# Second attention: the scores of two heads issued together on the two halves of TensorE's rows

## The chip, the cores and the metric

The kernel runs on one NeuronCore of a Trainium2 chip. The time is the device time of one execution in microseconds (us), the median of three runs. Everything is float32 at the inputs and outputs.

## The reference

Two transformer blocks in a row on 256 tokens of width 1024. The first has a short convolution, a feed-forward layer, a latent attention (MLA) and another feed-forward layer. The second, whose mixer is touched here, projects the tokens to a gated linear attention (GLA) and to a grouped-query attention (GQA), and goes on with a mixture of 64 experts. Cut to the part that matters:

```python
ATT_HEADS, ATT_KV_HEADS, ATT_HEAD_DIM = 8, 2, 64     # heads 0..3 share key head 0, heads 4..7 key head 1

def gqa_group(q, k, v, q_gain, k_gain, out_gain):
    qh = rms_norm_2(heads(q), q_gain); kh = rms_norm_2(heads(k), k_gain); vh = heads(v)
    qh = apply_axial_rope(qh, cos, sin) * (dh ** -0.5); kh = apply_axial_rope(kh, cos, sin)
    s = einsum('bkgqd,bksd->bkgqs', qb, kh)           # per head: 256 x 256 scores, no mask
    p = softmax(s, axis=-1)
    o = einsum('bkgqs,bksd->bkgqd', p, vh)
    return rms_norm_2(o.reshape(B, T, 512), out_gain)

h = h + concat(gla_group(...), gqa_group(...)) @ w_out
h = h + hier_moe(rms_norm_2(h, norm2_gain), ...)      # 64 experts, 3 matrices of 2 MB each
return rms_norm_2(h, final_gain)
```

## The kernel before, in words

Each engine has one instruction queue, written out by hand, and runs it in order. Engines meet only at semaphores. TensorE is PE, VectorE DVE, ScalarE ACT, GpSimd POOL; all large loads are issued by SyncE (SP), in a fixed order too.

The queries of the second attention lie transposed in SBUF: 128 partitions by four blocks of 256 tokens. Block `c` holds head `c` in partitions 0 to 63 and head `c + 4` in partitions 64 to 127. The keys lie in `KT` the same way, key head 0 in the lower half of the partitions and key head 1 in the upper. `slot(hd)` gives block and half of a head. A "head" below is the loop's number t or v; it runs from 0 to 7.

For each head the work is a chain over three engines:

1. `scores(t)` (PE, L1673): two matmuls, 64 rows deep, 256 columns wide, into PSUM bank `t % 2`. So two heads' scores can exist at once.
2. the maxima (DVE, L1828 and L1829), a reduction over both token tiles and a scaling; they signal `amax`.
3. the exponentials (ACT, L1768), one for each token tile with the row sums beside; they signal `aexps`, which also frees the bank.
4. `turned` (PE, L1682): four transposes of the probabilities into bank 2, and their copy to SBUF (ACT, L1780), which signals `apt_read`.
5. `weighted` (PE, L1691): four matmuls with the values into bank 3. After four heads DVE divides by the sums (L1806, L1808) and signals `oa`; the fifth head's `weighted` waits for that.

In PE's loop (`gqa_pe`) iteration t waits for `aexps` of t, then issues `scores(t + 1)`, `turned(t - 1)` and `weighted(t - 2)`.

The GLA's work is written in between these steps, on all engines. On PE: `gla_kv_pe` (L1394) in iteration 2, which waits for a copy on ACT (L1785); `gla_own_pe` (L1403), which waits for DVE's states (L1635, L1639), and `gla_past_pe` (L1418) in iteration 3; `gla_out_pe` (L1426), which waits for DVE's gated output, in iteration 6. On ACT, iteration 4 has the exponentials of head 4, then the copy of what `gla_past_pe` left (L1774, "past_read"), then the copy of head 3's probabilities, then eight squares (L1790), which wait for DVE's sum (L1650, "osum"). On DVE, iteration 4 has the maximum of head 4, then the low part of an output weight (`pair_lo(0)`, L268), then that sum (L1650), which waits for "past_read". DVE's iteration 6 has the maximum of head 6, then the GLA means (L1815), the gated output (L1821), and the division for the first four heads.

From iteration 7 on PE also computes the output projection (`part_out`, L317 to L319), which needs the GLA's operand from DVE and ACT (L564, L556). Its completed parts free the weight slots.

SP issues the experts' weights (2 MB each, `moe_sp`, L2179) in the order of slots 0, 3, 7, 2, 1, 4, 5, 8, 6, 9, each after a wait for the slot's last reader: slot 2 waits for "osum", slot 1 for the first output-projection part (`used` of `part_out(0, 0, 1)`), slot 4 for the last transposes of `turned_on`. After these the queue refills a slot whenever PE has read it.

Of the kernel before, what the change touches and what calls it, by code (L numbers as in the profile page):

```python
# [16 lines left out]
ALU = mybir.AluOpType  # L17
# [3 lines left out]
P = 128  # L21
T = 256
# [15 lines left out]
AH, AKV, AD = 8, 2, 64  # L38
# [81 lines left out]
def program(nc, a, consts_d, out):  # L120
    sems, chained = {}, {}

    def s(name):
        name = chained.get(name, name)
        if name not in sems:
            sems[name] = nc.alloc_semaphore(name)
        return sems[name]
# [38 lines left out]
    def sb(name, shape, dt=F32):  # L166
        return nc.alloc_sbuf_tensor(name, shape, dt)
# [39 lines left out]
    work = sb("work", [P, WORK])  # L207
    h = sb("h", [P, TT, D])
    small = sb("small", [P, 248])
# [24 lines left out]
    def wk(at, n):  # L234
        assert at + n <= WORK
        return work[:, at:at + n]

    def bank(b, n=512, at=0):
        return ps[:, b, at:at + n]
# [185 lines left out]
    def dve_step(dve, ins):  # L425
        steps["dve"] += 1
        ins.then_inc(s("dve_steps"), 1)
        dve.wait_ge(s("dve_steps"), steps["dve"])
# [858 lines left out]
    GQ, GK, GV, SG, ZT, QK, AV = 2048, 2560, 3072, 4096, 5120, 5632, 6912  # L1287
# [368 lines left out]
    QT, KT, PB2, PT2, OA, ON = 0, ZT, 1024, 2048, 3072, 0  # L1656

    def xw(at, n):

        return x_slots[:, at:at + n]  # L1660

    def slot(hd):

        return hd % 4, hd // 4

    P_BANK, O_BANK, OG_BANK, ON_BANK = 2, 3, 4, 0

    def gqa_pe(pe):
        def scores(t):
            c, par = slot(t)  # L1670
            rows = slice(64 * par, 64 * par + 64)
            for tt in range(TT):
                last = pe.matmul(bank(t % 2, T, T * tt), xw(QT, 1024)[rows, T * c + P * tt:T * c + P * tt + P],  # L1673
                                 work[rows, KT:KT + T], start=True, stop=True, skip_group_check=True)
            last.then_inc(s("ascores"), 1)

        def turned(v):
            if v:
                pe.wait_ge(s("apt_read"), v)
            for kk in range(TT):  # L1680
                for tt in range(TT):
                    last = pe.transpose(bank(P_BANK, P, T * kk + P * tt), xw(PB2 + 512 * (v % 2) + T * tt + P * kk, P), ident)  # L1682
            last.then_inc(s("aprobs_T"), 1)

        def weighted(v):
            pe.wait_ge(s("apt_read"), v + 1)
            if v == 4:
                pe.wait_ge(s("oa"), 1)
            for tt in range(TT):
                for kk in range(TT):  # L1690
                    last = pe.matmul(bank(O_BANK, AD, T * tt + AD * (v % 4)), xw(PT2 + 512 * (v % 2) + T * kk + P * tt, P),  # L1691
                                     wk(AV + P * kk + AD * (v // 4), AD), start=kk == 0, stop=kk == 1, skip_group_check=True)
            last.then_inc(s("aatt"), 1)

        def w_out(q):
            by_token(pe, U_WOUT + q, ACC, oT, [2 * q, 2 * q + 1], 2, D, 512, q == 0, q == 3,
                     between=first_rows(pe, "mix", "n2") if q == 3 else None).then_inc(s("used"), 1)

        def part_out(q, tt, part):
            unit_ready(pe, U_WOUT + q)  # L1700
            hi, lo = weights(U_WOUT + q, 2, D)
            cs = slice(512 * part, 512 * part + 512)
            for i, ch in enumerate((2 * q, 2 * q + 1)):
                last = passes(pe, ACC[tt][part], oT[0][:, ch, tt * P:(tt + 1) * P], oT[1][:, ch, tt * P:(tt + 1) * P],
                              hi[:, i, cs], lo[:, i, cs], q == i == 0, False)
            return last

        def turned_on():
            pe.wait_ge(s("on"), 1)
            for c in range(4):  # L1710
                for tt in range(TT):
                    last = pe.transpose(bank(ON_BANK + c // 2, P, (c % 2) * T + P * tt), xw(ON + 512 * tt + P * c, P), ident)
                if c % 2:
                    last.then_inc(s("on_T"), 1)

        pe.wait_ge(s("akt"), 1)
        scores(0)
        scores(1)
        gla_scores_pe(pe)
        gla_keys_pe(pe)  # L1720
        keep_busy(pe, 2, P_BANK)
        for t in range(1, AH + 1):
            pe.wait_ge(s("aexps"), t)
            if t + 1 < AH:
                scores(t + 1)
            if t == 2:
                gla_kv_pe(pe)
            turned(t - 1)
            if t == 6:
                gla_out_pe(pe)  # L1730
            if t >= 2:
                weighted(t - 2)
            if t == 3:
                gla_own_pe(pe)
                gla_past_pe(pe)
            if t == 7:
                pe.wait_ge(*mark("og_lo", 1))
                pe.wait_ge(*mark("past_read", 1))
                part_out(0, 1, 0)
        part_out(0, 1, 1)  # L1740
        weighted(AH - 1)
        pe.wait_ge(*mark("og_lo", 2))
        part_out(0, 0, 0)
        part_out(0, 0, 1).then_inc(s("used"), 1)
        part_out(1, 1, 0)
        part_out(1, 1, 1)
        turned_on()
        part_out(1, 0, 0)
        part_out(1, 0, 1).then_inc(s("used"), 1)
        pe.wait_ge(*mark("mo_lo", 2))  # L1750
        w_out(2)
        w_out(3)
# [47 lines left out]
    def gqa_dve(dve):  # L1800
        def weighted(half):

            dve.wait_ge(s("aatt"), 4 * half + 4)
            sums = small[:, 128 + 16 * half:144 + 16 * half].rearrange("p (h c) -> p h c", c=4)[:, :, 2:4]
            inv = small[:, 112 + 8 * half:120 + 8 * half].rearrange("p (h c) -> p h c", c=2)
            dve_step(dve, dve.reciprocal(inv, sums))  # L1806
            for tt in range(TT):
                last = dve.tensor_tensor(xw(OA + 512 * tt + 256 * half, 256).rearrange("p (h c) -> p h c", c=AD),  # L1808
                                         bank(O_BANK, T, T * tt).rearrange("p (h c) -> p h c", c=AD),
                                         inv[:, :, tt:tt + 1].broadcast_to([P, 4, AD]), ALU.mult)  # L1810
            last.then_inc(s("oa"), 1)

        def gla_mean(tt):
            dve.wait_ge(*mark("g_ssq", tt + 1))
            dve.tensor_scalar(small[:, 72 + 4 * tt:76 + 4 * tt], small[:, 64 + 4 * tt:68 + 4 * tt], 1.0 / DV, EPS, ALU.mult, ALU.add)\  # L1815
                .then_inc(s("all_mean"), 1)

        def gated(tt):
            dve.wait_ge(*mark("g_rstd", tt + 1))
            for q in range(4 * tt, 4 * tt + 4):  # L1820
                last = dve.scalar_tensor_tensor(wk(OG + P * q, P), wk(OSUM + P * q, P), small[:, 80 + q:81 + q],  # L1821
                                                wk(SG + P * q, P), ALU.mult, ALU.mult)
            last.then_inc(s("og"), 1)

        for t in range(AH):
            m = 128 + 4 * t
            dve.wait_ge(s("ascores"), t + 1)
            dve_step(dve, dve.tensor_reduce(small[:, 210 + 2 * t:212 + 2 * t], bank(t % 2).rearrange("p (t n) -> p t n", t=2), AX, ALU.max))  # L1828
            dve.tensor_scalar(small[:, m:m + 2], small[:, 210 + 2 * t:212 + 2 * t], -(AD ** -0.5), None, ALU.mult).then_inc(s("amax"), 1)  # L1829
            if t == 1:  # L1830
                gla_masked_dve(dve)
            if t == 3:
                gla_states_dve(dve)
            if t == 4:
                pair_lo(dve, 0)
                gla_sum_dve(dve)
            if t >= 5 and t < 7:
                gla_mean(t - 5)
            if t == 6:
                for tt in range(TT):  # L1840
                    gated(tt)
                weighted(0)
        operand_dve(dve, "og", [(OG_BANK, 2), (OG_BANK + 1, 2)], lambda k: col("gla_out"), oT)
        pair_lo(dve, 1)
        weighted(1)
        pair_lo(dve, 2)
        dve.wait_ge(*mark("a_ssq", 1))
        rstd_dve(dve, "a", [(164, 2, 512)], 166, 2)
        for tt in range(TT):
            last = dve.tensor_scalar(xw(ON + 512 * tt, 512), xw(OA + 512 * tt, 512), small[:, 168 + tt:169 + tt], None, ALU.mult)  # L1850
        last.then_inc(s("on"), 1)
        operand_dve(dve, "mo", [(ON_BANK, 2), (ON_BANK + 1, 2)], lambda k: col("att_out", k), oT, first=4)
# [910 lines left out]
```

## Time and profile before

| | |
|---|---|
| median of 3 runs | 1597.17 us (1596.48 to 1597.68) |
| span of the profiled execution | 1594.4 us |
| median less that span | 2.8 us |
| PE busy | 1301.5 us (82%) |
| DVE busy | 540.8 us (34%) |
| ACT busy | 444.9 us (28%) |
| DMA, mean over the span | 326 GB/s |
| chain that ended last | DMA 49%, PE 45% |

The profile is of one execution. Its own time is the span, from the first to the last instruction; some 2.8 us lie around it when it is held against the median of the runs. A row of the timeline reads: start, duration, engine, line, operation, operands, shapes, count; in brackets the idle time of the engine before it and who ended it. A matmul of float32 shows as two records, so `x4` in the timeline is two matmul calls of the order. Several instructions in a row are merged into one line.

### The profile page before, as it was taken

What the parts mean: (1) busy time and instruction counts of PE and PEld (TensorE: products, weight loads), DVE (VectorE), ACT (ScalarE), POOL (GpSimd) and SP (SyncE); (2) the same over time, 40 slices, a digit from 0 to 9 for tenths busy, and PEclk for the clock granted to TensorE, in tenths of its full rate; (3) what the DMA queues carried; (4) which work ended last, traced back from release to release, by engine and by line L of the source; (5) the groups of instructions that cost most, each with busy time, mean ns of one, the idle gap of its engine ahead of it and who ended that gap; (6) DMA issues with size and microseconds to landing.
All of it is one profiled execution on the core that took longest, in us unless ns stands there. A gap on an engine that the chain in (4) does not pass through costs nothing.

```text
span 1594.4 us, 29664 instructions
## 1 busy us (share of the span) xinstructions
PE 1301.5 (82%) x12728; PEld 973.2 (61%) x12728; DVE 540.8 (34%) x911; ACT 444.9 (28%) x760; POOL 60.9 (4%) x84
## 2 busy tenths in 40 slices
PE   8999999999999999999676677666666667677666
PEld 8989999878999987876344344334333334334333
DVE  6666555776655578641000101001010010010001
ACT  5454444655444457522011011011011011011011
POOL 3000000001000025000000000000000000000000
PEclk9999999999999999999889889989998889879887
DMA  9555554444555536499999999999999999999997
GB/s 354 202 183 185 184 196 152 155 156 138 193 184 204 181 124 261 190 425 428 431 431 432 431 432 432 432 431 431 432 430 432 432 431 432 431 432 432 432 431 308
DMA packets 46214, 519.39 MB, mean 326 GB/s; under 512 B 5583, under 2 KB 5844, under 8 KB 8660
## 3 DMA queue, kind: packets, MB, share of 16 engines
q1 hardware_dynamic: 44928, 517.34, 79.5%
q0 software_dynamic: 896, 0.99, 0.3%
q8 instruction: 36, 0.59, 0.1%
q10 hardware_dynamic: 340, 0.35, 0.1%
q14 instruction: 14, 0.11, 0.0%
HBM read 517.61 MB, written 1.05 MB: 325 GB/s over the span
## 4 chain that ended last, share of the span: by engine, by line
DMA 49%; PE 45%; DVE 3%; ACT 2%; issue 1%; SPq 0%; POOL 0%; ACTq 0%; POOLq 0%; DVEq 0%
DMA work<-in_moe_units 48%; PE ps L317 11%; PE ps L319 11%; PE ps L318 11%; PE ps L2260 5%; PE ps L2251 1%; PE ps L990 1%; PE ps L989 0%; ACT w_split L276 0%; PE ps L484 0%; DVE xT_lo L564 0%; DVE w_split L280 0%; PE ps L1691 0%; DMA work<-in_conv_w 0%; PE ps L2294 0%
## 5 line engine op out<-in xcount | busy, mean ns | idle before, releaser
L2251 PE MATMUL ps<-ring,work 128*32 128x256 f32 x2976 | 202.9, 419 | 91.6 <-DMA ring<-in_moe_units 91.6
L2466 DVE TENSOR_TENSOR work<-ps,work 128x128 f32<-128x128 f32 x64 | 18.7, 292 | 738.8 <-ACT work L2379 738.8
L317 PE MATMUL ps<-xT_hi,w_split 128*128 128x256 f32 x960 | 266.5, 278 | 1.4 <-DVE xT_lo L564 1.4
L318 PE MATMUL ps<-xT_lo,w_split 128*128 128x256 f32 x960 | 265.4, 276 | 0.0
L319 PE MATMUL ps<-xT_hi,w_split 128*128 128x256 f32 x960 | 265.3, 276 | 0.0
L280 DVE TENSOR_TENSOR w_split<-ring,w_split 128x2048 fp32r<-128x2048 f32 (+3 forms) x101 | 227.9, 2259 | 92.4 <-ACT w_split L276 91.2
L276 ACT ACTIVATE w_split<-ring 128x2048 fp32r<-128x2048 f32 (+3 forms) x105 | 196.3, 1872 | 143.4 <-PE ps L319 143.3
L2251 PEld LDWEIGHTS ps<-ring,work 128*32 128x32 f32 x2976 | 95.3, 118 | 189.4 <-DMA ring<-in_moe_units 118.5
L317 PEld LDWEIGHTS ps<-xT_hi,w_split 128*128 128x128 f32 x960 | 180.2, 188 | 3.6 <-issue 2.5
L318 PEld LDWEIGHTS ps<-xT_lo,w_split 128*128 128x128 f32 x960 | 180.4, 188 | 0.9
L319 PEld LDWEIGHTS ps<-xT_hi,w_split 128*128 128x128 f32 x960 | 180.3, 188 | 0.0
L2251 PE MATMUL ps<-x_slots,work 128*32 128x256 f32 x1024 | 85.0, 489 | 67.1 <-DMA x_slots<-in_moe_units 67.1
L2260 PE MATMUL ps<-ring,work 128*32 128x256 f32 x992 | 74.3, 449 | 54.0 <-DMA ring<-in_moe_units 54.0
L2260 PE MATMUL ps<-work 128*32 128x256 f32 x960 | 72.9, 455 | 55.2 <-DMA work<-in_moe_units 55.2
L2378 ACT ACTIVATE work<-ps 128x256 f32<-128x256 f32 x64 | 24.6, 384 | 319.1 <-PE ps L2285 319.1
L2385 ACT ACTIVATE work<-ps 128x256 f32<-128x256 f32 x63 | 24.2, 384 | 294.1 <-PE ps L2260 294.1
L2251 PEld LDWEIGHTS ps<-x_slots,work 128*32 128x32 f32 x1024 | 37.1, 134 | 111.7 <-DMA x_slots<-in_moe_units 83.2
L319 PE MATMUL ps<-w_split,xS_lo 128*128 128x512 f32 (+1 forms) x230 | 89.7, 390 | 0.0
L317 PE MATMUL ps<-w_split,xS_hi 128*128 128x512 f32 (+1 forms) x230 | 89.0, 387 | 0.7 <-DVE xS_lo L564 0.7
L318 PE MATMUL ps<-w_split,xS_hi 128*128 128x512 f32 (+1 forms) x230 | 89.2, 388 | 0.0
L2260 PEld LDWEIGHTS ps<-ring,work 128*32 128x32 f32 x992 | 39.3, 124 | 80.5 <-issue 71.3
L2260 PEld LDWEIGHTS ps<-work 128*32 128x32 f32 x960 | 38.3, 126 | 82.2 <-issue 72.5
(372 smaller groups left out, 1566.8 us busy)
## 6 DMA issues: line engine op xcount, KB each, us to landing
ring<-in_moe_units SPq DMA_DIRECT2D x124, 2048.0 KB, 26.8
ring<-in_ffn_units SPq DMA_DIRECT2D x66, 1024.0 KB, 4.8
x_slots<-in_moe_units SPq DMA_DIRECT2D x32, 2048.0 KB, 25.7
work<-in_moe_units SPq DMA_DIRECT2D x32, 2048.0 KB, 26.9
ring<-in_conv_units SPq DMA_DIRECT2D x15, 1024.0 KB, 11.8
ring<-in_win_units SPq DMA_DIRECT2D x9, 1024.0 KB, 4.8
ring<-in_wo_units SPq DMA_DIRECT2D x4, 1024.0 KB, 4.9
kept_slot<-in_moe_units SPq DMA_DIRECT2D x2, 2048.0 KB, 14.7
```

Source lines behind the costliest of these rows:

```text
L276: act.activation(w_split[:, u % SPLIT, 0, 0:n], raw[:, u % RAW, 0:n], ACT.Copy).then_inc(s("hi_done"), 1)
L280: dve.tensor_tensor(w_split[:, u % SPLIT, 1, 0:n], raw[:, u % RAW, 0:n], w_split[:, u % SPLIT, 0, 0:n].bitcast(F32), ALU.subtract).then_in ...
L317: pe.matmul(out_ap, stat_hi, mov_hi, start=first, stop=False, skip_group_check=True)
L318: pe.matmul(out_ap, stat_hi, mov_lo, start=False, stop=False, skip_group_check=True)
L319: return pe.matmul(out_ap, stat_lo, mov_hi, start=False, stop=last, skip_group_check=True)
L990: last = pe.matmul(o, work[r, QPT + T * (t // 2) + P * tt:QPT + T * (t // 2) + P * tt + P], work[r, KPT:KPT + n], start=False, stop=True, ...
L2251: last = pe.matmul(ps[CAP * j:CAP * j + CAP, b, 0:BLK], xstat[:, 4 * half + k, CAP * lane:CAP * lane + CAP], w[k][:, j // 2, BLK * (j % 2) ...
L2260: last = pe.matmul(ps[CAP * j:CAP * j + CAP, b, 0:BLK], astat[par][:, k % 2, k // 2, :], w[:, k, BLK * j:BLK * j + BLK], start=k == 0, sto ...
L2378: act.activation(wk(ST + 256 * par, 256), bank(b, 256, 256), ACT.Copy)
L2385: act.activation(wk(YS + BLK * par, BLK), bank(b, BLK), ACT.Copy).then_inc(s("y_out"), 1)
L2466: dve.tensor_tensor(astat[par], bank(b, 256).rearrange("p (c s j m) -> p c s j m", c=2, s=2, j=2)[:, :, 1, :, :], wk(SI, 128).rearrange("p ...
```

## The change

The heads are taken in the order 0, 4, 1, 5, 2, 6, 3, 7. `scores(pair)` issues both heads of a block at once: for each token tile one matmul on the lower 64 rows into bank 0 and one on the upper 64 rows into bank 1. A single `ascores` count stands for both, and the next pair is issued only in even iterations, after the exponentials of both heads. The maxima wait for the pair's count. `weighted` picks the value half by `v % 2`, and the division writes its four heads to their places in two strides. The number of matmuls is the same.

```diff
-    def slot(hd):
-
-        return hd % 4, hd // 4
-
     def gqa_pe(pe):
-        def scores(t):
-            c, par = slot(t)
-            rows = slice(64 * par, 64 * par + 64)
+        def scores(pair):
             for tt in range(TT):
-                last = pe.matmul(bank(t % 2, T, T * tt), xw(QT, 1024)[rows, T * c + P * tt:T * c + P * tt + P],
-                                 work[rows, KT:KT + T], start=True, stop=True, skip_group_check=True)
+                q0 = T * pair + P * tt
+                for par in range(2):
+                    rows = slice(64 * par, 64 * par + 64)
+                    last = pe.matmul(bank(par, T, T * tt), xw(QT, 1024)[rows, q0:q0 + P], work[rows, KT:KT + T],
+                                     start=True, stop=True, skip_group_check=True)
             last.then_inc(s("ascores"), 1)
...
         pe.wait_ge(s("akt"), 1)
         scores(0)
-        scores(1)
...
         for t in range(1, AH + 1):
             pe.wait_ge(s("aexps"), t)
-            if t + 1 < AH:
-                scores(t + 1)
+            if t % 2 == 0 and t < AH:
+                scores(t // 2)
...
         for t in range(AH):
             m = 128 + 4 * t
-            dve.wait_ge(s("ascores"), t + 1)
+            dve.wait_ge(s("ascores"), t // 2 + 1)
```

On PE, around the GLA's large blocks (iterations 2 to 5), before:

```order
L1394 MATMUL ps<-work 64x128 x24
L1682 MATMUL ps<-cst,x_slots 128x128 x4
L1691 MATMUL ps<-work,x_slots 128x64 x4
L1673 MATMUL ps<-work,x_slots 128x256 x2
L1682 MATMUL ps<-cst,x_slots 128x128 x4
L1691 MATMUL ps<-work,x_slots 128x64 x4
L1403 MATMUL ps<-work 128x128 x16
L1418 MATMUL ps<-work 64x128 x24
L1673 MATMUL ps<-work,x_slots 128x256 x2
```

and in the changed kernel, where L1670 is `scores`, L1679 `turned` and L1688 `weighted`:

```order
L1394 MATMUL ps<-work 64x128 x24
L1679 MATMUL ps<-cst,x_slots 128x128 x4
L1688 MATMUL ps<-work,x_slots 128x64 x4
L1679 MATMUL ps<-cst,x_slots 128x128 x4
L1688 MATMUL ps<-work,x_slots 128x64 x4
L1403 MATMUL ps<-work 128x128 x16
L1418 MATMUL ps<-work 64x128 x24
L1670 MATMUL ps<-work,x_slots 128x256 x4
```

The scores of the loop's head 4 stood ahead of L1403 and L1418; now they stand behind both, together with those of head 5.

On PE, around iteration 6 and the GLA's output (L1426), before:

```order
L1673 MATMUL ps<-work,x_slots 128x256 x2
L1682 MATMUL ps<-cst,x_slots 128x128 x4
L1691 MATMUL ps<-work,x_slots 128x64 x4
L1673 MATMUL ps<-work,x_slots 128x256 x2
L1682 MATMUL ps<-cst,x_slots 128x128 x4
L1426 MATMUL ps<-cst,work 128x128 x8
```

and now:

```order
L1679 MATMUL ps<-cst,x_slots 128x128 x4
L1688 MATMUL ps<-work,x_slots 128x64 x4
L1670 MATMUL ps<-work,x_slots 128x256 x4
L1679 MATMUL ps<-cst,x_slots 128x128 x4
L1426 MATMUL ps<-cst,work 128x128 x8
```

The scores of head 6 were issued one iteration earlier than those of head 7; now both come after the wait for the exponentials of head 5. The order of the instructions on DVE, ACT, POOL and SP is the same in both kernels.

## Rows read from the trace of the kernel before

**Rows 1.** The page: the chain that ended last, by engine.
```profile
DMA 49%; PE 45%; DVE 3%; ACT 2%; issue 1%; SPq 0%; POOL 0%; ACTq 0%; POOLq 0%; DVEq 0%
```

**Rows 2.** Windows: length, busy us of PE, PEld, DVE, ACT, POOL; clock, DMA, GB/s.
```profile
649.00:663.00 14.00, 13.35 (x92) 11.28 (x90) 10.73 (x28) 12.95 (x40) 2.11 (x2) 1.00 0.41 150
...
666.75:1578.00 911.25, 641.58 (x7994) 374.42 (x7992) 95.85 (x345) 110.96 (x345) 1.81 (x3) 0.89 1.01 430
```

**Rows 3.** Timeline of SP's queue, slots 2, 1 and 4.
```profile
650.91 0.33 SPq L2179 DMA_DIRECT2D work<-in_moe_units  x1
666.75 0.33 SPq L2179 DMA_DIRECT2D ring<-in_moe_units  x1
670.35 0.33 SPq L2179 DMA_DIRECT2D x_slots<-in_moe_units  x1
```

**Rows 4.** Timeline: the scores of heads 0 and 1.
```profile
628.29 1.99 PE L1673 MATMUL ps<-work,x_slots 64*128 64x256 f32 x8
```

**Rows 5.** The chain that ended last, in order of time: start, us, what.
```profile
711.73 1.08 PE ps L2294 x16
```

**Rows 6.** Timeline, PE, iterations 1 to 4.
```profile
633.38 1.13 PE L1673 MATMUL ps<-work,x_slots 64*128 64x256 f32 x4 [0.47 <-ACT x_slots L1768]
...
634.44 0.66 PE L1682 MATMUL ps<-cst,x_slots 128*128 128x128 f32 x4
...
642.91 3.79 PE L1403 MATMUL ps<-work 128*128 128x128 f32 x32
...
646.63 1.69 PE L1418 MATMUL ps<-work 64*64 64x128 f32 x48
```

**Rows 7.** Timeline, ACT and DVE, iterations 1 to 3.
```profile
634.03 0.22 ACT L1768 ACTIVATION_READ_ACCUMULATOR x_slots<-ps,small 128x1 f32 x1
...
635.63 1.02 ACT L1785 ACTIVATE work<-ps 128x1024 f32<-128x1024 f32 x1
...
640.13 2.28 DVE L1639 SCALAR_TENSOR_TENSOR work<-work,ps 128x128 f32<-128x128 f32 x8
```

**Rows 8.** Timeline, DVE and ACT, iterations 4 and 5.
```profile
642.33 0.68 DVE L1828 TENSOR_REDUCE small<-ps 128x2 f32<-128x512 f32 x1
...
643.12 2.28 DVE L268 TENSOR_TENSOR w_raw<-ring,w_raw 128x2048 fp32r<-128x2048 f32 x1
643.25 0.47 ACT L1768 ACTIVATE x_slots<-ps,small 128x256 f32<-128x256 f32 x1 [0.38 <-DVE small L1829]
...
644.07 0.20 ACT L1768 ACTIVATION_READ_ACCUMULATOR x_slots<-ps,small 128x1 f32 x1
...
648.41 1.02 ACT L1774 ACTIVATE work<-ps 128x1024 f32<-128x1024 f32 x1 [4.14 <-PE ps L1418]
...
649.46 1.42 DVE L1650 TENSOR_TENSOR work<-ps,work 128x256 f32<-128x256 f32 x4 [4.06 <-ACT work L1774]
...
650.50 0.30 ACT L1790 ACTIVATE work<-work 128x128 f32<-128x128 f32 x1
...
652.84 0.46 ACT L1768 ACTIVATE x_slots<-ps,small 128x256 f32<-128x256 f32 x1
```

**Rows 9.** Timeline, from the gated output to the output projection.
```profile
653.10 2.39 DVE L1821 SCALAR_TENSOR_TENSOR work<-work,small 128x128 f32<-128x128 f32 x8
...
655.63 0.76 DVE L1808 TENSOR_TENSOR x_slots<-ps,small 128x256 f32<-128x256 f32 x2
...
658.70 0.47 PE L317 MATMUL ps<-w_raw,oT_hi 128*128 128x512 f32 x1
```

**Rows 10.** Windows around two idle stretches of PE, columns as in rows 2.
```profile
758.00:760.00 2.00, 0.01 (x1) 0.00 (x0) 0.69 (x1) 0.00 (x0) 0.00 (x0) 1.00 1.06 440
760.00:763.00 3.00, 1.93 (x32) 1.13 (x32) 0.00 (x0) 0.39 (x1) 0.00 (x0) 1.00 1.01 433
773.00:776.00 3.00, 0.32 (x11) 0.12 (x8) 0.00 (x0) 0.38 (x1) 0.00 (x0) 1.00 1.02 431
776.00:780.00 4.00, 2.92 (x32) 1.39 (x31) 0.00 (x0) 0.38 (x1) 0.00 (x0) 0.58 1.00 426
```

More of the change, by code:

```diff
@@ L1691, in weighted @@
                     last = pe.matmul(bank(O_BANK, AD, T * tt + AD * (v % 4)), xw(PT2 + 512 * (v % 2) + T * kk + P * tt, P),
-                                     wk(AV + P * kk + AD * (v // 4), AD), start=kk == 0, stop=kk == 1, skip_group_check=True)
+                                     wk(AV + P * kk + AD * (v % 2), AD), start=kk == 0, stop=kk == 1, skip_group_check=True)
             last.then_inc(s("aatt"), 1)
@@ L1804, in weighted @@
             sums = small[:, 128 + 16 * half:144 + 16 * half].rearrange("p (h c) -> p h c", c=4)[:, :, 2:4]
-            inv = small[:, 112 + 8 * half:120 + 8 * half].rearrange("p (h c) -> p h c", c=2)
-            dve_step(dve, dve.reciprocal(inv, sums))
+            inv = small[:, 112 + 8 * half:120 + 8 * half]
+            dve_step(dve, dve.reciprocal(inv.rearrange("p (h c) -> p h c", c=2), sums))
             for tt in range(TT):
-                last = dve.tensor_tensor(xw(OA + 512 * tt + 256 * half, 256).rearrange("p (h c) -> p h c", c=AD),
-                                         bank(O_BANK, T, T * tt).rearrange("p (h c) -> p h c", c=AD),
-                                         inv[:, :, tt:tt + 1].broadcast_to([P, 4, AD]), ALU.mult)
+                last = dve.tensor_tensor(xw(OA + 512 * tt, 512).rearrange("p (r q c) -> p q r c", r=2, c=AD)[:, 2 * half:2 * half + 2],
+                                         bank(O_BANK, T, T * tt).rearrange("p (q r c) -> p q r c", r=2, c=AD),
+                                         inv.rearrange("p (q r c) -> p q r c", r=2, c=2)[:, :, :, tt:tt + 1].broadcast_to([P, 2, 2, AD]), ALU.mult)
             last.then_inc(s("oa"), 1)
```

## The prediction

> **What bounds the kernel now.** I read the chain that ended last first. It splits nearly evenly, DMA 49% and PE 45% [rows 1], so the question is where it passes from one to the other. The windows answer that: from 666.75 us to 1578 us the DMA share is full at 430 GB/s while PE is busy for 642 of 911 us [rows 2]. This is the stream of expert weights, and its bytes are fixed. What moves the end is therefore when that full stretch begins, and SP's queue shows it: after slot 2 at 650.91 the queue stands until 666.75, when slot 1 is free, and 3.6 us later slot 4 follows [rows 3]. A 2 MB load takes 4.9 us at 430 GB/s, so slot 2's load is long over by 666.75 and slot 1's still runs when slot 4 is issued. Slot 1 is freed by the first part of the output projection on PE. Every us that this part comes later or earlier shifts the end by one, as long as everything behind it shifts alike, and behind it PE's work (the rest of the projection, the router) is unchanged. Slot 2 has some 10 us of idle DMA behind its load and may slip by some us without harm.
>
> Ahead of 666.75 PE is nearly full, 13.35 of 14 us [rows 2]. So PE's work counts there, but only while PE stays fed.
>
> **Part 1: the matmuls themselves.** Heads 0 and 1 lay on the same half of the rows; their four calls take 1.99 us [rows 4], against 1.13 for two [rows 6], so 0.43 for one more call. No row shows the pair form. Its bounds: no overlap, 1.99 us for a pair; full overlap, 1.13. The nearest row is L2294, 256 columns, 32 rows deep, going round four row groups and four banks: 16 records (8 calls) in 1.08 us, 0.135 a call [rows 5]. That is three times as quick as 0.43, so groups of rows do run side by side with 256 columns into different banks. I take 1.13 us for a pair. PE gets 0.86 us less work for each of four pairs, 3.4 in all. The first pair's share is worth nothing: DVE reaches its first maximum only after its own GLA products.
>
> The Trainium skill (TensorEngine Tiling (Array Packing), PSUM Bottleneck under Performance Considerations) warns that tiling speeds up TensorE but not the evacuation of PSUM, and that the latter may become the bottleneck. The rows bear this out for a pair: 1.13 us on PE, but on DVE 0.92 for each head's maxima up to the start of its exponentials (642.33 to 643.25), and on ACT 1.02 for each head's exponentials (643.25 to 644.27) [rows 8]. By the rule alone nothing would be gained; the sum below goes by the rows and comes out worse than that.
>
> **Part 2: iterations 1 to 3, earlier.** Iteration 1 has no scores any more, so turned(0), which began at 634.44, can begin where the scores did, at 633.38 [rows 6]. ACT is through with head 1's exponentials at 634.25 [rows 7], copies turned(0), then the GLA copy L1785, now from 634.62 instead of 635.63 [rows 7]: 1.01 us earlier. The pair's scores fit ahead of it (634.30 to 635.43). L1394 on PE and DVE's states, which wait for it, come 1.01 earlier: the states end at 641.40 instead of 642.41 [rows 7]. Iteration 3 lost its scores too, another 1.06, so PE could be 2.07 earlier at L1403 (642.91 [rows 6]) and waits for the states instead: with 0.05 for the hand-over and 0.06 for the load of the weights it starts at 641.51, 1.40 us earlier. L1403 and L1418 take what they took. Call the end of L1418 X: 648.32 before (646.63 + 1.69 [rows 6]), 646.92 now. With free overlap there is nothing more to gain here, since the states are the limit.
>
> **Part 3: the first new wait.** Head 4's scores used to be issued at 640.52, before X; now they are issued behind it. DVE waits for them in iteration 4, and behind that maximum stand pair_lo(0) and the sum L1650. ACT waits for the maximum, and behind head 4's exponentials stand the copy L1774 and the squares L1790. All four used to be done with that before X (head 4's exponentials ended at 644.27) [rows 8]. Now, in us after X: scores end 1.06 (they start 0.07 before X), maximum and scaling end 1.99, pair_lo(0) from 1.90 to 4.18 (2.28 long), exponentials end 3.05, L1774 from 2.94 to 3.96, L1650 from 4.18 (pair_lo(0) is last), its first half (of 1.42) 0.75 later, so the squares start at 4.93. Before they started at 650.50, X + 2.18, so this costs 2.75. The squares take 2.34, up to 652.84 [rows 8]; now they end at X + 7.27.
>
> **Part 4: the second new wait.** DVE's iteration 6 has head 6's maximum ahead of the gated output. Its scores stood ready before the squares ended; now they wait for head 5's exponentials, which come behind the squares. After the squares: exponentials 1.00, scores 0.05 + 1.13, maximum and scaling with their hand-overs 0.98. The gated output L1821 starts at X + 10.43. Before it started at 653.10, X + 4.78 [rows 9]. The difference is 5.65; less the 1.40 by which X is earlier: 4.25 us later, at 657.35.
>
> **Part 5: from there to the stream.** The gated output and the division took from 653.10 to 656.39 [rows 9]: now 657.35 to 660.64. PE then does head 4's weighted, which waits for the division, turned(6) and head 5's weighted, and 2.3 us after the division the projection began, at 658.70 [rows 9]; now at 662.9, 4.2 later. PE was full from here to the freeing of slot 1, so that comes at 670.95. The division's output in two strides has the same 256 elements for each instruction; I take nothing for it (bounds: 0 and, if its 0.76 us doubled, +0.8). The new copies, waits for `apt_read` and exponentials of heads 6 and 7 fit beside this.
>
> Between row-tiled and whole-array work PE loses time: turned begins 1.06 us after scores (633.38 to 634.44 [rows 6]), though two calls at 0.43 would do with 0.86. The Trainium skill (TensorEngine Tiling (Array Packing), Key Properties) says that a change of tiling mode drains the engine; here half the changes go. Three fewer changes of some 0.2 us lie in the stretches where PE now waits, so I leave the sum as it is; with the rule's drains counted in full it would be 0.6 less.
>
> **Sum.** -1.40 + 2.75 + 2.90 = +4.25, 4.2 at slot 1. Against the profiled execution: 1594.4 + 4.2 = 1598.6 of span; with the 2.8 us around it, 1601.4 against the median of 1597.17.
>
> **Rivals.**
> - The clock falls as well. In the new waits PE stands idle for about 2.2 us (649.2 to 651.4), 2.5 us (652.7 to 655.2) and, but for four transposes, 2.8 us (657.0 to 659.8). In the trace an idle stretch of about 2 us from 758 left the granted clock at 1.00; one of 2.7 us, from 773 to 776, was followed by a mean of 0.58 over 4 us, which is 3.4 of the 4 at the half clock, 1.2 GHz [rows 10]. If it happens here, 3.4 us of PE's time do 1.7 us of work: +1.7 on top, 1603.1.
> - The halves do not overlap. Then pairs 2 and 3 cost 0.86 more each and X is 0.5 later: +6.4, 1603.6. Against it stands L2294 [rows 5].
> - Only the first wait shows, because head 5's exponentials or head 6's maximum come out of the way: 4.2 - 2.9 = +1.3, 1598.5, no change that can be told. Against it: both are queued in order.
> - Faster: PE stays the engine that decides. It was full [rows 2]; if maxima and exponentials are hidden behind it as before, three pairs give back 3 x 0.86 = 2.6 us and three fewer changes of tiling 0.6: slot 1 is free at 663.5 and the kernel takes 1594.0. It needs head 4's exponentials not to hold L1774 by more than PE's saving; the decisive point is 0 on the sum of Parts 2 to 4.
>
> **How the numbers follow.** Forecast 0.56; clock 0.14; no overlap 0.06; one wait only 0.14; faster 0.10. What a measurement can tell is 0.2%, 3.2 us: 1600.4 and 1594.0 are the edges. The forecast is 1 us over the upper one, so I give a tenth of its own share and all of "one wait only" to no change, as well as half of the last rival, whose 1594.0 lies on the lower edge: slower 0.50 + 0.14 + 0.06 = 0.70, same 0.06 + 0.14 + 0.05 = 0.25, faster 0.05. The range of 8 in 10 leaves out most of the faster case and the far tail: 1597.0 to 1604.5; the forecast's own is 1600.2 to 1602.8.
>
> **What would show it.** The scores L1670 take about 1.1 us for each pair of eight records. L1770 (the old L1774) starts 2.9 us after the GLA's L1418 instead of 0.1 after it. The squares start about 4.9 after it. L1817 (gated) starts near 657.4, and PE has idle stretches ended by ACT and DVE between 649 and 660. SP issues slot 1 near 671 and the DMA share is full from there. If slot 1 is issued at or before 666.75 the forecast is wrong from Part 3 on; if it is issued late and the end does not move, the reading of the bound is wrong.

## The result and the profile after

The changed kernel takes 1606.1 us (1605.66 to 1607.48, four runs) against 1596.83 us for the kernel before in the same comparison: a ratio of 1.0058, 95% interval 1.0046 to 1.007. It is slower by 9.3 us where 4.2 were forecast, and above the range, which ended at 1604.5. The profiled executions differ by as much: spans of 1603.8 and 1594.4 us.

The timeline of SP's queue in the changed kernel shows where. The first four rows are slots 3, 2, 1 and 4; the last three of these answer [rows 3]. The fifth row is slot 3 in the kernel before.

```profile
628.89 0.33 SPq L2175 DMA_DIRECT2D x_slots<-in_moe_units  x1
...
652.98 0.33 SPq L2175 DMA_DIRECT2D work<-in_moe_units  x1
676.00 0.33 SPq L2175 DMA_DIRECT2D ring<-in_moe_units  x1
679.60 0.33 SPq L2175 DMA_DIRECT2D x_slots<-in_moe_units  x1
...
628.39 0.33 SPq L2179 DMA_DIRECT2D x_slots<-in_moe_units  x1
```

Slot 1 is issued at 676.00 instead of 666.75, 9.25 us later, and that is the whole loss. The windows of the changed kernel (length, busy us of PE, PEld, DVE, ACT, POOL, then clock, DMA share, GB/s) say that nothing is lost or given back behind it: from there the stream runs for 911.3 us at 430 GB/s, as it did [rows 2].

```profile
649.00:652.00 3.00, 0.92 (x9) 0.78 (x7) 2.97 (x5) 2.42 (x6) 0.00 (x0) 1.00 0.00 0
652.00:656.00 4.00, 2.19 (x14) 2.04 (x16) 1.79 (x6) 3.67 (x21) 1.02 (x1) 0.61 0.53 139
...
652.50:653.00 0.50, 0.50 (x7) 0.50 (x5) 0.50 (x3) 0.50 (x5) 0.00 (x0) 0.88 0.00 0
...
656.00:662.00 6.00, 4.80 (x20) 3.06 (x20) 3.96 (x15) 1.78 (x7) 1.04 (x1) 0.50 0.60 257
662.00:670.00 8.00, 8.00 (x34) 7.18 (x32) 4.68 (x8) 4.77 (x10) 0.00 (x0) 0.50 0.00 1
670.00:674.00 4.00, 4.00 (x28) 3.58 (x26) 0.74 (x3) 2.40 (x2) 0.00 (x0) 1.00 0.00 0
...
676.00:1587.30 911.30, 642.08 (x7994) 374.09 (x7992) 95.92 (x345) 110.97 (x345) 1.81 (x3) 0.89 1.01 430
```

The clock column is what the forecast's sum did not have: 0.61 over 4 us and 0.50 over the next 14, which is about 17 us at 1.2 GHz. In the kernel before it stood at 1.00 from 649 to 663 [rows 2], and from there to 666.75 as well. The half us from 652.5 says when it fell: a mean of 0.88 is 0.12 us at the half at its end, so the fall is at about 652.9. PE had then worked again for 0.9 us.

The waits themselves are where they were forecast. From the timeline of the changed kernel, one row for each step; the attention's own lines (from L1764 on) had numbers four higher on DVE and ACT, and three higher on PE.

```profile
641.97 3.84 PE L1403 MATMUL ps<-work 128*128 128x128 f32 x32 [0.47 <-DVE work L1639]
...
645.73 1.69 PE L1418 MATMUL ps<-work 64*64 64x128 f32 x48
...
647.36 1.13 PE L1670 MATMUL ps<-work,x_slots 64*128 64x256 f32 x8
...
648.54 0.69 DVE L1824 TENSOR_REDUCE small<-ps 128x2 f32<-128x512 f32 x1 [6.63 <-PE ps L1670]
...
650.38 1.02 ACT L1770 ACTIVATE work<-ps 128x1024 f32<-128x1024 f32 x1
...
652.04 0.63 PE L1679 MATMUL ps<-cst,x_slots 128*128 128x128 f32 x4 [2.12 <-ACT x_slots L1776]
...
652.33 0.31 ACT L1786 ACTIVATE work<-work 128x128 f32<-128x128 f32 x1 [0.43 <-DVE work L1650]
...
655.73 2.08 PE L1670 MATMUL ps<-work,x_slots 64*128 64x256 f32 x8 [1.77 <-ACT x_slots L1764]
...
657.86 0.69 DVE L1824 TENSOR_REDUCE small<-ps 128x2 f32<-128x512 f32 x1 [4.03 <-PE ps L1670]
...
658.73 2.38 DVE L1817 SCALAR_TENSOR_TENSOR work<-work,small 128x128 f32<-128x128 f32 x8
...
666.31 0.77 PE L317 MATMUL ps<-w_raw,oT_hi 128*128 128x512 f32 x1
```

Everything ahead of the attention came 0.50 us later in this execution (slot 3 at 628.89, before at 628.39), so times are best counted from slot 3. The forecast's times are counted from 628.39. The last column is the first experiment, described below.

| us after slot 3 | before | forecast | after | e1_filler |
|---|---|---|---|---|
| L1403 starts | 14.52 | 13.12 | 13.08 | 13.07 |
| L1418 ends (X) | 19.93 | 18.53 | 18.53 | 18.53 |
| past_read copy starts | 20.02 | 21.47 | 21.49 | 21.48 |
| squares start | 22.11 | 23.46 | 23.44 | 23.43 |
| gated output starts | 24.71 | 28.96 | 29.84 | 29.16 |
| projection starts | 30.31 | 34.51 | 37.42 | 34.76 |
| slot 1 issued | 38.36 | 42.56 | 47.11 | 42.80 |

Up to the squares the sum holds to 0.05 us. It parts company at the third pair's scores, which take 2.08 us instead of 1.13: the clock has fallen.

### The profile page after: what moved, and what is told of

The parts are those of the page before. It is cut to its first block, busy times and chain, and to the rows that moved or that the text cites. A ratio compares the mean times of both kernels' runs of the same rounds, so it can differ in the third digit from the quotient of the medians.

```text
span 1603.8 us, 29666 instructions
## 1 busy us (share of the span) xinstructions
PE 1304.7 (81%) x12728; PEld 975.0 (61%) x12728; DVE 538.8 (34%) x911; ACT 444.8 (28%) x760; POOL 63.5 (4%) x84
## 4 chain that ended last, share of the span: by engine, by line
DMA 48%; PE 45%; DVE 3%; ACT 2%; issue 1%; POOL 0%; SPq 0%; ACTq 0%; POOLq 0%; DVEq 0%
DMA work<-in_moe_units 48%; PE ps L317 11%; PE ps L319 11%; PE ps L318 11%; PE ps L2256 5%; PE ps L2247 1%; PE ps L990 1%; DVE w_split L280 1%; PE ps L989 0%; ACT w_split L276 0%; PE ps L484 0%; DVE xT_lo L564 0%; PE ps L1688 0%; DMA work<-in_conv_w 0%; PE ps L2290 0%
```

## Experiments

All were run against the kernel before on the same chip; "before" beside each is its median there. Where a change of some tenths is read, it is from the distance between slot 3 and slot 1.

**e1_filler: keep the clock up.** The changed kernel, with matmuls on zeros where PE waits.

```diff
             if t == 2:
                 gla_kv_pe(pe)
+            if t == 5:
+                keep_busy(pe, 8, 0)
             turned(t - 1)
             if t == 6:
+                keep_busy(pe, 9, 4)
                 gla_out_pe(pe)
             if t >= 2:
                 weighted(t - 2)
+            if t == 5:
+                keep_busy(pe, 9, 0)
```

> The changed kernel with 26 whole-array matmuls on zeros written into the three places where PE waits (8 and 9 around turned(4) in iteration 5, 9 ahead of the GLA output in iteration 6), each group some 2 us long, into banks that nobody uses there. They compute nothing that is used. Theory A (the new waits cost 4.2 us, and the half clock from 652 to 670 us costs the other 4.5 to 5): the clock stays at 1.00, slot 1 is issued 4.2 to 4.8 us after where it was before instead of 9.3, and the time is 1601 to 1602 us. Rival B (the waits cost all 9.3 us and the clock is only a witness, since PE waits anyway): the clock stays up and the time stays at 1606. If the fillers are too long they delay PE by some tenths of a us.

Measured: 1601.63 us against 1597.16, ratio 1.0028 (1.0016 to 1.0039). Its timeline shows the second filler and the third pair's scores behind it, at full speed, then the gated output (L1822 here) and the start of the projection; SP's queue shows slots 3 and 1; its windows show the clock.

```profile
654.18 2.33 PE L324 MATMUL ps<-zeros 128*128 128x512 f32 x9
656.44 1.13 PE L1670 MATMUL ps<-work,x_slots 64*128 64x256 f32 x8
...
658.49 2.38 DVE L1822 SCALAR_TENSOR_TENSOR work<-work,small 128x128 f32<-128x128 f32 x8
...
664.09 0.47 PE L317 MATMUL ps<-w_raw,oT_hi 128*128 128x512 f32 x1
```

```profile
629.33 0.33 SPq L2180 DMA_DIRECT2D x_slots<-in_moe_units  x1
...
672.13 0.33 SPq L2180 DMA_DIRECT2D ring<-in_moe_units  x1
```

```profile
649.00:670.00 21.00, 19.79 (x126) 16.63 (x126) 14.43 (x34) 14.93 (x44) 2.06 (x2) 1.00 0.28 101
```

Slot 1 comes 42.80 us after slot 3: 4.44 later than before, against 4.20 forecast, and 4.31 sooner than in the changed kernel, which differs by work that computes nothing. So the loss of 9.25 us between the two profiled executions is 0.50 ahead of slot 3, 4.44 of waits, and 4.31 of clock. The medians say the same: 4.5 us above the kernel before with the filler, 9.3 without. The fillers are not quite free. Counted from slot 3 the third pair's scores start 0.27 us later than in the changed kernel (27.11 against 26.84), since the second filler is still running, so the waits alone may be 4.2 and the clock 4.5 (an estimate). Rival B is out.

**e7_filler_first: fill the first idle stretch alone.** Of the three additions above only `keep_busy(pe, 8, 0)` ahead of `turned(4)`.

> The changed kernel with the zero matmuls in the first of the three idle stretches alone (8 of them, ahead of turned(4)). Theory A1 (the first idle stretch, 2.2 us before 652, is what the clock fell after): the clock stays up until the second and third stretches of about 2 us; if neither is followed by a fall, the time is that with all three filled, 1601.6. Theory A2 (any of the three suffices): the clock falls later, around 656 to 660, and the time is between 1603 and 1606.

Measured: 1604.68 us (1601.06 to 1605.74, four runs) against 1596.85, ratio 1.0042 (1.0027 to 1.0058). The profiled execution is near the changed kernel, slot 1 at 46.66. Its windows:

```profile
653.00:656.00 3.00, 1.35 (x13) 1.21 (x11) 1.21 (x5) 3.00 (x21) 1.02 (x1) 1.00 0.53 120
656.00:660.00 4.00, 3.09 (x12) 1.88 (x12) 1.73 (x7) 1.41 (x7) 0.72 (x1) 0.57 1.00 430
660.00:663.00 3.00, 1.77 (x12) 1.33 (x13) 2.85 (x9) 1.65 (x6) 0.32 (x1) 1.00 0.02 5
663.00:666.00 3.00, 3.00 (x17) 3.00 (x17) 1.73 (x5) 2.58 (x8) 0.00 (x0) 0.51 0.00 0
```

The clock now holds until 656, falls behind the second stretch, comes back at 660 and falls again behind the third. So the first stretch was not the only one that can bring it down (A2); filling one saved little in this execution. The four runs lie at 1601.06, 1603.96, 1605.4 and 1605.74, and the profiled one is the slowest. The quickest is as quick as e1_filler (1601.41 to 1603.49), so in it the clock may have stayed up, as A1 has it; no trace of that run exists. The spread of 4.7 us looks as if the clock did one thing behind these stretches in some executions and another in others.

**e2_order_only, e2_again: the order of the heads alone.** Single heads' scores, issued where they used to be.

```diff
-        def scores(pair):
+        def scores(t):
+            pair, par = t // 2, t % 2
...
-            if t % 2 == 0 and t < AH:
-                scores(t // 2)
+            if t + 1 < AH:
+                scores(t + 1)
...
-            dve.wait_ge(s("ascores"), t // 2 + 1)
+            dve.wait_ge(s("ascores"), t + 1)
```

> Only the order of the heads is changed (0, 4, 1, 5 ...), with the value halves and the strided division that go with it; scores are issued one head at a time where they were before the change. Theory A (the loss is the place of the scores in the queue): the time of before, 1596.8 us, within 1 us; neighbouring heads on different halves may overlap where they follow each other. Rival C (the strided division, or the alternation of the row halves, costs something): 1 us or more above before.

Measured first: 1599.37 us, but from 1596.17 to 1605.83, against 1597.16 (ratio 1.0018, 1.0003 to 1.0034). Slots 3 and 1 in its profile:

```profile
631.23 0.33 SPq L2176 DMA_DIRECT2D x_slots<-in_moe_units  x1
...
669.62 0.33 SPq L2176 DMA_DIRECT2D ring<-in_moe_units  x1
```

38.39 us, as before; what this execution was late by lies ahead of slot 3, in instructions that are the same.

> The kernel with the order of the heads alone once more. In its first run slot 1 was issued 38.39 us after slot 3, against 38.36 before, and what it was late by (2.8 us) lay ahead of slot 3, in code that is the same. Theory A: again 38.4 us between the two; the median is within 1 us of before, unless the scatter ahead of the attention belongs to this binary. Rival C (the order costs): more than 39 us between the two.

Measured again: 1596.88 against 1596.85 us, ratio 1.0001 (0.9992 to 1.001); the two issues at 630.67 and 669.05, 38.38 apart. The order of the heads, the value halves and the strided division cost nothing that can be told; Rival C is out. What made the first round's upper runs slow was not found.

**e3_pair_before_gla: take away the first wait.**

```diff
-            if t == 3:
+            if t == 4:
                 gla_own_pe(pe)
                 gla_past_pe(pe)
```

> The changed kernel with gla_own and gla_past moved on PE from iteration 3 to the end of iteration 4, so that the scores, transposes and weighted of iteration 4 stand ahead of them. Theory A: the first new wait (2.75 us) goes, since heads 4 and 5 have their scores before the GLA's last products; these start some 1.7 us later instead, because iteration 4 now stands ahead of them. The second wait (2.9 us) stays. Sum against before: -1.40 + 1.7 + 2.9 = +3.2 us, 1600.0 with a full clock; PE still idles twice for more than 2 us, so up to 4.5 us of half clock on top, 1604.5. DVE's maximum of head 4 no longer waits 6.6 us. Rival D (the first wait was not on the path): 1606 or more, by the 1.7 us 1607.8.

Measured: 1604.26 us against 1597.16, ratio 1.0043 (1.0028 to 1.0057). The copy L1770 again follows L1418 by 0.1 us, the wait of 6.63 us on DVE is 0.70, and the third pair's scores wait and run slowly as before:

```profile
643.33 0.69 DVE L1824 TENSOR_REDUCE small<-ps 128x2 f32<-128x512 f32 x1 [0.70 <-PE ps L1670]
...
648.26 1.69 PE L1418 MATMUL ps<-work 64*64 64x128 f32 x48
...
650.04 1.02 ACT L1770 ACTIVATE work<-ps 128x1024 f32<-128x1024 f32 x1 [4.76 <-PE ps L1418]
...
655.29 2.08 PE L1670 MATMUL ps<-work,x_slots 64*128 64x256 f32 x8 [2.12 <-ACT x_slots L1764]
```

The gated output starts 28.69 us after slot 3, 1.15 sooner than in the changed kernel although L1418 ends 1.8 us later. Slot 1 is at 44.84: 6.48 later than before. If the queues cost the 3.2 that were forecast, 3.3 are left for the clock, inside what was expected; the run does not separate the two. Rival D is out: the first wait was on the path.

**e4_gated_first: take away the second wait.**

```diff
+            if t == 6:
+                gla_mean(1)
+                for tt in range(TT):
+                    gated(tt)
             dve.wait_ge(s("ascores"), t // 2 + 1)
...
-            if t >= 5 and t < 7:
-                gla_mean(t - 5)
+            if t == 5:
+                gla_mean(0)
             if t == 6:
-                for tt in range(TT):
-                    gated(tt)
                 weighted(0)
```

> The changed kernel with DVE's queue changed in iteration 6: the GLA's second mean and the gated output stand ahead of the maximum of head 6 instead of behind it; nothing else. Theory A: the gated output no longer waits for head 6's scores and starts 2.9 us sooner; the division still stands behind the maximum, so PE's head 4 gains 2.0 us. Against before +4.2 - 2.0 = +2.2 us, 1599.0 with a full clock, up to 4.5 more if it falls: 1603.5. Rival E (the second wait is hidden behind the slow clock and gives nothing): 1606.

Measured: 1600.55 us against 1597.16, ratio 1.002 (1.001 to 1.0029). Slot 1 is at 42.15, 3.79 later than before. The GLA's output on PE follows turned(5) without a wait, and the clock comes back between 661 and 662 (windows 660:661 and 661:662):

```profile
657.63 1.11 PE L1679 MATMUL ps<-cst,x_slots 128*128 128x128 f32 x4
658.53 1.92 PE L1426 MATMUL ps<-cst,work 128*128 128x128 f32 x8
660.24 1.54 PE L1688 MATMUL ps<-work,x_slots 128*128 128x64 f32 x8
661.62 0.61 PE L1679 MATMUL ps<-cst,x_slots 128*128 128x128 f32 x4
```

```profile
660.00:661.00 1.00, 1.00 (x8) 1.00 (x6) 0.35 (x3) 1.00 (x4) 0.00 (x0) 0.50 0.00 0
661.00:662.00 1.00, 1.00 (x9) 1.00 (x10) 1.00 (x3) 1.00 (x5) 0.00 (x0) 0.82 0.00 0
```

Of 8.75 us (from slot 3) one move in DVE's queue gave back 4.96. Of that, 2.0 were forecast for the wait. The rest fits the shorter slow stretch, about 7 us (654.5 to 661.4) instead of 17, but no run takes this move with the waits filled, so the split is not shown. Rival E is out.

**e5_both: both moves together.** The two diffs above in one kernel.

> The two moves of before together: gla_own and gla_past behind iteration 4 on PE, and the gated output ahead of head 6's maximum on DVE. Theory A: both waits are gone from the GLA's chain; left are 0.4 us (L1403 later than before), and 0.9 us because head 6's maximum now stands between the gated output and the division, with up to 1 us on the operand's ACT step behind head 6's exponentials: +1.3 to +2.3 us at slot 1, counted from slot 3's issue, 1598 to 1599.5 with a full clock. PE still idles about 1.8 us before turned(4) and about 2.1 us before the third pair's scores, so the clock may fall; then 1 to 4 us on top. Rival F (something else of the pair form costs): above 1601 at full clock.

Measured: 1599.11 us against 1596.85, ratio 1.0014 (1.0005 to 1.0023); slot 1 at 40.57, 2.21 later than before. The granted clock was 0.73 over 650 to 655 and 0.58 over 655 to 660, which is some 7 us at the half.

```profile
650.00:655.00 5.00, 2.16 (x16) 1.96 (x18) 3.76 (x13) 4.40 (x23) 2.13 (x2) 0.73 0.53 144
655.00:660.00 5.00, 5.00 (x29) 4.26 (x26) 3.77 (x12) 2.63 (x9) 0.00 (x0) 0.58 0.64 275
```

That is inside Theory A's 1.3 to 2.3 us, which were for a full clock; the 1 to 4 us that a fall was to add on top did not come in full, as only 0.9 are left above 1.3. Rival F is out: even with the clock low the time is under 1601.

**e6_early: arrange all queues around the pairs.**

```diff
-            if t == 6:
-                gla_out_pe(pe)
...
-            if t == 3:
+            if t == 4:
                 gla_own_pe(pe)
                 gla_past_pe(pe)
-            if t == 7:
-                pe.wait_ge(*mark("og_lo", 1))
-                pe.wait_ge(*mark("past_read", 1))
-                part_out(0, 1, 0)
+        gla_out_pe(pe)
+        pe.wait_ge(*mark("og_lo", 1))
+        pe.wait_ge(*mark("past_read", 1))
+        part_out(0, 1, 0)
...
-            if t == 4:
+            if t == 5:
                 pair_lo(dve, 0)
                 gla_sum_dve(dve)
...
+            if t == 7:
+                weighted(0)
+                gla_mean(0)
+                gla_mean(1)
+                for tt in range(TT):
+                    gated(tt)
```

On ACT past_read and the squares move from iteration 4 to 5, and the GLA's operand from 6 to 7.

> The pair form with all queues arranged around it. PE: gla_own and gla_past behind iteration 4, the GLA output behind iteration 8. ACT: the exponentials of heads 4 and 5 ahead of past_read, squares behind it, the GLA operand in iteration 7. DVE: maxima of heads 4 and 5 ahead of pair_lo(0) and the sum, those of heads 6 and 7 and the first division ahead of the GLA means and the gated output. Theory A: no engine waits for scores any more; the gated output comes about 0.6 us later after L1418's end than before, but transposes and weighted of heads 6 and 7 fill the wait for it (1.3 us), and part_out starts with only head 7's weighted behind it: slot 1 about 1 to 1.5 us earlier than in the kernel before, 1595.5, if the clock stays up. Rival G (the pair form gives nothing, since what PE saves is lost in the transposes' single bank): 1597 or more.

Measured: 1600.94 us (1596.9 to 1602.36) against 1596.85, ratio 1.0021 (1.0011 to 1.003). Theory A's 1595.5 was too optimistic, and the median hides two groups: three of the ten runs took 1596.9 to 1597.1, the other seven 1600.5 to 1602.4. The profiled one is of the slower group (1600.57), with slot 1 at 41.70. Its timeline and its clock over 654 to 655 and 655 to 660 show why:

```profile
651.39 0.66 PE L1679 MATMUL ps<-cst,x_slots 128*128 128x128 f32 x4
654.24 1.34 PE L1688 MATMUL ps<-work,x_slots 128*128 128x64 f32 x8 [2.19 <-DVE x_slots L1802]
655.38 1.06 PE L1679 MATMUL ps<-cst,x_slots 128*128 128x128 f32 x4
...
660.28 1.74 PE L1426 MATMUL ps<-cst,work 128*128 128x128 f32 x8
```

```profile
654.00:655.00 1.00, 0.76 (x7) 0.79 (x7) 0.24 (x3) 1.00 (x5) 0.75 (x1) 0.95 0.80 344
655.00:660.00 5.00, 5.00 (x26) 5.00 (x26) 2.19 (x8) 1.24 (x5) 1.24 (x2) 0.50 0.64 275
```

PE waits 2.19 us for the division, after 12 us of work without a gap. 0.7 us behind this one wait, at about 654.9, the clock falls, and five steps, most of them at half speed, now stand ahead of the GLA's output, whose input was ready at 657.5 (L1815 on DVE, 655.30 and 2.19 long). The quicker group left no trace; that its clock stayed up is likely, not shown. So Rival G's number (1597 or more) came, but here with the clock, which its reason, the transposes' single bank, does not need.

**e8_early_filled: the same with that stretch filled.**

```diff
             turned(t - 1)
+            if t == 6:
+                keep_busy(pe, 8, 6)
...
+            if t == 7:
+                gla_out_pe(pe)
-        gla_out_pe(pe)
```

> The queues of e6_early with two changes: 8 zero matmuls on PE in iteration 6 behind turned(5), where PE stood idle for 2.2 us waiting for the division, and the GLA output in iteration 7 ahead of turned(7) instead of behind the loop. In e6_early the clock fell at about 655 us, behind that idle stretch, and the GLA output started 2.8 us after its input was ready, behind transposes and weighted at half speed. Theory A: the clock stays at 1.00; the GLA output starts at about 657.5 (counted with slot 3 issued at 628.6) and the projection at 659.6, with only weighted of head 7 left inside it: slot 1 is issued 37.7 to 38.4 us after slot 3, against 38.36 in the kernel before, so 1596.0 to 1597.0 us, a tie or a gain too small to be told. Rival H (the pair form has a cost of its own at full clock): slot 1 more than 39.5 us after slot 3, 1598 or more.

Measured: 1596.66 us against 1597.0, ratio 0.9997 (0.9988 to 1.0006). Slots 3 and 1:

```profile
628.45 0.33 SPq L2176 DMA_DIRECT2D x_slots<-in_moe_units  x1
...
666.40 0.33 SPq L2176 DMA_DIRECT2D ring<-in_moe_units  x1
```

37.95 us, 0.41 less than before, with the clock at 1.00 throughout. No difference that the runs can tell. The pair form has no cost of its own (Rival H is out), and with the waits filled it gives nothing to speak of: slot 1 is 0.41 us earlier for the 3.4 us that four pairs take off PE. The GLA's chain over the other engines sets the pace here. The gated output waits 1.06 us for POOL, and the operand's low half (L564) 1.40 us for L556, with which ACT reads PSUM; PE's projection then waits 0.34 us for L564.

The Trainium skill (TensorEngine Tiling (Array Packing), PSUM Bottleneck) says that the reading of PSUM may become the limit once tiling has made TensorE quicker. This run agrees in its outcome, but does not single that reading out, since POOL is waited for as well.

**e9_halves_in_turn: is it the alternation?** e1_filler with the loops inside `scores` exchanged.

```diff
-            for tt in range(TT):
-                q0 = T * pair + P * tt
-                for par in range(2):
+            for par in range(2):
+                for tt in range(TT):
+                    q0 = T * pair + P * tt
```

> e1_filler (the changed kernel with all three idle stretches filled) with the two loops inside scores exchanged: both token tiles of the lower half first, then both of the upper, instead of alternating. Same matmuls, same banks. Theory A (neighbouring calls on different halves run side by side): only the middle two of four calls can still overlap, a block takes 1.5 to 2.0 us instead of 1.13, and since two of the blocks stand in the new waits, slot 1 comes 0.8 to 1.7 us later than in e1_filler: 1602.4 to 1603.3. Rival I (the queue reorders or the order does not matter): blocks of 1.13 us and 1601.6.

Measured: 1601.68 us against 1597.0, ratio 1.0029 (1.0017 to 1.0041); slot 1 at 42.88 (e1_filler 42.80). The blocks take as long as with alternation:

```profile
646.93 1.14 PE L1670 MATMUL ps<-work,x_slots 64*128 64x256 f32 x8
```

I expected 1.5 to 2.0 us. Rival I holds as to the time, and the trace shows the two halves side by side here too. The first row counts the matmuls of `scores` that are under way in a stretch near the start of the first block; the second is the same in the kernel before, where both heads lie on one half. (Columns: length, PE, PEld, clock, DMA share, GB/s.)

```profile
628.36:628.60 0.24, 0.24 (x2) 0.24 (x4) 1.00 1.91 819
...
628.30:628.60 0.30, 0.30 (x1) 0.28 (x2) 1.00 1.76 710
```

A call is two records, and a record does not say on which half it ran. But two have started here within 0.02 us of the block's start (628.34), where on one half the second starts over 0.3 us after the first (628.29). So the second one here belongs to the upper half, although the program has both calls of the lower half ahead of it. Whether the engine starts it early or the order was changed before the program reached the chip is not shown.

## Why the prediction was wrong

- The bound (fixed stream of weights behind slot 1) was right: the issue moved 9.25 us, the span 9.4.
- Part 1, the pair in 1.13 us: right, 1.13 measured at full clock, against the 1.99 that both heads took on one half [rows 4].
- Part 2, -1.40 us: right; X came 1.40 us earlier, counted from slot 3.
- Part 3, +2.75: right; the squares start 4.91 us after X, forecast 4.93.
- Part 4, +2.90: right when the clock is up. In e1_filler the gated output starts at X + 10.63, forecast 10.43. The 0.2 are those of the third pair's scores, which start at X + 8.58 (656.44) behind the zero matmuls, where the sum had 8.32. In the changed kernel itself, without them, they start at X + 8.31.
- Part 5, 4.2 at slot 1: right, 4.44 in e1_filler, and from the gated output to slot 1 it takes as long as before (13.64 and 13.65 us).
- **The step that failed** is the rival "the clock falls as well", in its chance (0.14) and its price (+1.7). Its signs were all read: three idle stretches of 2.2 to 2.8 us, and rows in which about 2 us left the clock up and 2.7 brought it down [rows 10]. The sum itself had nothing for the clock. Two mistakes were made.
  - First, the length of a stretch was taken to decide. One of the three, 2.8 us but for four transposes, was longer than the 2.7 that had brought the clock down, so 0.14 was low even by these rows. And the runs show falls behind shorter ones. In the changed kernel PE stands idle for 2.12 us up to 652.04, and the clock falls at about 652.9, before the second stretch begins. In e6_early it falls 0.7 us after a single stretch of 2.19 us, and in e7_filler_first behind one of 1.80. The stretch in rows 10 that left it up was as long, 2.15. So the length alone does not tell, and the runs of e6_early and of e7_filler_first differ by some 5 us among themselves. What tells such stretches apart stays open.
  - Second, the price was taken from rows in which the clock was low for 3.4 of 4 us. Here it was low for some 17 us: it fell behind 3 us in which PE was busy for 0.92, and stayed low while PE was busy for 2.19 of 4 and 4.80 of 6, with two more idle stretches (1.8 us up to 655.73 and 1.1 up to 659.91); then PE worked for all of 8 us before it was back. Against e1_filler that made the gated output 0.68 us later, the projection 2.66 and slot 1 4.31, where 1.7 had been put. Against the forecast's own 42.56 for slot 1 it is 4.55.
- The Trainium skill (TensorE: Matmul & The Clock Gate, HAM oscillation) describes short bursts of matmuls between waits for DMA that bring the clock down again and again. e7_filler_first agrees, with 0.57, 1.00 and 0.51 in turn, though its waits are for ACT and DVE.
- The rivals "no overlap" and "faster" were rightly small. "One wait only" was wrong: in e1_filler, at full clock, the squares and the gated output both come as late as the sum has them, and e3 and e4 each take one wait away and move slot 1, though partly by way of the clock.

## What to carry to other kernels

Before a block of issued work is made twice as large, list what stands behind its consumers in every in-order queue: here heads 4 to 7 waited at two places, and each held up a chain that had nothing to do with them. New waits of about 2 us on PE are to be priced with the clock as well, for all the work that follows until it is back; in this kernel that doubled the loss, though a stretch as long left the clock up elsewhere in the same kernel. Matmuls on zeros in the waits are a cheap way to tell the cost of the waits from that of the clock, and they give the second back.

## What was not expected of the hardware

- The granted clock stayed at 1.2 GHz through 8.00 us in which PE was busy without a gap (662 to 670), after 10 us of broken work. In e4_gated_first PE worked without a gap from 655.62, and by 661.62 its four transposes took 0.61 us again instead of 1.11.
- A stretch of 2.12 us without work brought the clock down in the changed kernel, and one of 2.15 us in the kernel before did not. One program may do either: e6_early has runs at 1596.9 and at 1602.4 us, though only one of them left a trace.
- Four 64-row matmuls on two halves take 1.14 us as a block, whether the halves alternate or follow each other; the same four on one half take 1.99. Matmuls of the two halves are under way together even when the program has them one half after the other.
- The profiled executions of these kernels differ by up to 2.8 us ahead of the attention (slot 3 at 628.4 to 631.2), with the same instructions there. The two latest are both of the kernel with the order of the heads alone, so this may go with the program and not only with the execution. A distance inside the profile is the better measure for edits of a few us behind that point.
